# Segment sums of the state-space heads as two fp32r products: decay steps split into a high and a low part, spread over the triangle by VectorE and GpSimd

## The reference, cut to what matters

```python
cs = jnp.cumsum(dt * a.reshape(g, r), axis=2)
seg = cs[:, :, :, None] - cs[:, :, None, :]
decay_in = jnp.exp(jnp.where(lower, seg, -jnp.inf))
cb = jnp.einsum('bcqgn,bcsgn->bcqsg', cm, bm)
m = cb[..., None] * decay_in * dt[:, :, None]
y_diag = jnp.einsum('bcqsgr,bcsgrp->bcqgrp', m, x)
```

## Time and profile before

| what | value |
|---|---|
| median of 3 runs | 3071.8 us (3071.16 to 3074.44) |
| the profiled execution, its own time | 3071.51 us |
| its span | 3069.9 us |
| mean granted clock of PE | 0.964 of 2.4 GHz |

### The profile page before, as it was taken

The page is one execution under the profiler, slowest core; times in us unless marked ns, Lnnn a source line. Parts: engine busy times, 40 slices in busy tenths (PEclk is TensorE's granted clock), DMA queues, the critical chain, the costliest instruction groups (busy, mean ns, idle before and its releaser), DMA issues. The chain is left out here.

```text
span 3069.9 us, 50804 instructions
## 1 busy us (share of the span) xinstructions
PE 2810.0 (92%) x17878; PEld 2411.9 (79%) x17878; DVE 2146.2 (70%) x4117; ACT 1531.7 (50%) x2880; POOL 178.6 (6%) x180
## 2 busy tenths in 40 slices
PE   5999588899997993999999999999999999999993
PEld 4988355566665873999999999999999999999992
DVE  3565666666665447787787788788788778788773
ACT  3543344444444332555555555555555555555552
POOL 0000011001100000000000000000000000000001
PEclk8999799999999995999999999999999999999996
DMA  6121301121222433877777787777688678677754
GB/s 249 65 64 56 114 23 45 50 93 64 85 82 102 160 130 131 258 243 232 247 242 226 242 254 222 235 247 239 221 254 241 219 245 250 222 247 240 230 190 174
DMA packets 359719, 547.40 MB, mean 178 GB/s; under 512 B 14785, under 2 KB 287937, under 8 KB 359617
## 3 DMA queue, kind: packets, MB, share of 16 engines
q1 hardware_dynamic: 350720, 514.59, 50.6%
q0 software_dynamic: 8896, 31.46, 4.3%
HBM read 493.51 MB, written 52.49 MB: 178 GB/s over the span
## 5 line engine op out<-in xcount | busy, mean ns | idle before, releaser
L2531 PE MATMUL banks<-rowsT_parts,weights_high 128*128 128x384 f32 x4096 | 1184.0, 361 | 12.3 <-DVE hidden_parts L2462 7.3
L2532 PE MATMUL banks<-rowsT_parts,weights_low 128*128 128x192 f32 x4096 | 1026.3, 251 | 0.0
L2531 PEld LDWEIGHTS banks<-rowsT_parts,weights_high 128*128 128x128 f32 x4096 | 770.0, 188 | 21.5 <-DVE hidden_parts L2462 9.9
L2532 PEld LDWEIGHTS banks<-rowsT_parts,weights_low 128*128 128x128 f32 x4096 | 783.4, 191 | 1.4
L2542 PE MATMUL banks<-weights_high,hidden_parts 128*128 128x512 f32 x1536 | 435.5, 392 | 0.0
L2449 DVE TENSOR_TENSOR gate_up_sums<-banks,gate_up_sums 128x192 f32<-128x192 f32 x512 | 181.6, 355 | 327.7 <-ACT gate_up_sums L2367 327.7
L2367 ACT ACTIVATE gate_up_sums<-banks 128x192 f32<-128x192 f32 x512 | 165.0, 322 | 452.2 <-PE banks L2532 448.2
L2542 PEld LDWEIGHTS banks<-weights_high,hidden_parts 128*128 128x128 f32 x1536 | 283.4, 188 | 69.9
L2542 PE MATMUL banks<-weights_low,hidden_parts 128*128 128x512 f32 (+1 forms) x1024 | 319.6, 393 | 0.0
L2399 DVE TENSOR_TENSOR weights_low<-slab_up,weights_high 128x1024 fp32r<-128x1024 f32 x256 | 311.9, 1218 | 0.0
L2399 DVE TENSOR_TENSOR weights_low<-slab_down,weights_high 128x1024 fp32r<-128x1024 f32 x256 | 311.5, 1217 | 0.0
(11 more groups left out here) (288 smaller groups left out, 3754.1 us busy)
## 6 DMA issues: line engine op xcount, KB each, us to landing
slab_gate<-w_gate SPq DMA_DIRECT2D x128, 1024.0 KB, 5.4
slab_up<-w_up SPq DMA_DIRECT2D x128, 1024.0 KB, 7.3
slab_down<-w_down SPq DMA_DIRECT2D x128, 1024.0 KB, 4.9
arena_attend<-w_ada SPq DMA_DIRECT2D x8, 2048.0 KB, 7.9
arena_attend<-ssd_tiles SPq DMA_DIRECT2D x12, 992.0 KB, 9.5
arena_inputs<-w_ada SPq DMA_DIRECT2D x4, 2048.0 KB, 12.2
ssd_tiles<-arena_inputs SPq DMA_DIRECT2D x24, 256.0 KB, 2.0
mixed<-arena_attend SPq DMA_DIRECT2D x12, 512.0 KB, 2.6
```

The lines of the kernel that those rows point to most:

```text
L2531: nc.tensor.matmul(out[:, 0:2 * CT], w_hi[:, u, block], x[:, k, :], start=k == 0, stop=False)
L2532: mm = nc.tensor.matmul(out[:, 0:CT], w_lo[:, u, block], x[:, k, 0:CT], start=False, stop=k == KD - 1)
```

## The change

- The decay steps of the next tile are split by DVE in turn 4 (`steps`): `step_hi` is `dta` rounded to fp32r (128x16), `step_lo` is `dta` minus `step_hi`.
- `terms` spreads both parts over the triangle, so each engine makes two tensors of 128x1024 where it made one, with fp32r as their output type. DVE makes the one of the high part in turn 6, where its only one was, and the one of the low part at the end of turn 7. POOL makes both one after the other, and waits for `steps_done` of the next tile where it waited for the tile's transfer.
- Each of the four segment sums is two fp32r products that add up in PSUM, high and low, with a copy of the triangles in fp32r as the stationary operand. The copy is made once at the start.
- `r_sum`, the triangles and the steps have memory of their own, and the shared area is 2048 columns smaller.

```diff
-    r_sum = A.at(A_R, 2, NS, P)
+    r_sum = core.once("decay_steps", [P, 2, 2, NS, P], F32R)
+    turns_r = core.once("triangles", [P, 2, P], F32R)
+    step_hi = core.once("steps_high", [P, 2, 16], F32R)
+    step_lo = core.once("steps_low", [P, 2, 16])
...
         def _(pool):
             def terms(g, j):
 
-                wait_apart(pool, tile_in[j], turn_of(g, j) + 16, pool_turns)
+                wait_apart(pool, steps_done, g + 1, pool_turns)
                 wait_apart(pool, seg_mm, g * 4, pool_turns)
-                nc.gpsimd.tensor_tensor(r_sum[:, 1], core.masks[:, M_GE, :].unsqueeze(1).broadcast_to([P, NS, P]),
-                                        dta[j][:, 8:16].unsqueeze(2).broadcast_to([P, NS, P]),
-                                        ALU.mult).then_inc(terms_b, 1)
+                for part, steps in enumerate((step_hi[:].bitcast(F32), step_lo[:])):
+                    ins = nc.gpsimd.tensor_tensor(r_sum[:, part, 1], core.masks[:, M_GE, :].unsqueeze(1).broadcast_to([P, NS, P]),
+                                                  steps[:, j, 8:16].unsqueeze(2).broadcast_to([P, NS, P]), ALU.mult)
+                ins.then_inc(terms_b, 1)
...
-            def terms(g, j):
+            def steps(g, j):
 
                 dve.wait_ge(tile_in[j], turn_of(g, j) + 16)
+                if not early(g):
+                    dve.wait_ge(terms_b, g - 1)
+                nc.vector.tensor_copy(step_hi[:, j], dta[j]).then_inc(steps_high, 1)
+                dve.wait_ge(steps_high, g + 3)
+                nc.vector.tensor_tensor(step_lo[:, j], dta[j], step_hi[:, j].bitcast(F32), ALU.subtract).then_inc(steps_done, 1)
+
+            def terms(g, j, part):
+                dve.wait_ge(steps_done, g + 1)
                 dve.wait_ge(seg_mm, g * 4)
-                nc.vector.tensor_tensor(r_sum[:, 0], core.masks[:, M_LE, :].unsqueeze(1).broadcast_to([P, NS, P]),
-                                        dta[j][:, 0:8].unsqueeze(2).broadcast_to([P, NS, P]),
-                                        ALU.mult).then_inc(terms_f, 1)
+                nc.vector.tensor_tensor(r_sum[:, part, 0], core.masks[:, M_LE, :].unsqueeze(1).broadcast_to([P, NS, P]),
+                                        (step_hi[:].bitcast(F32), step_lo[:])[part][:, j, 0:8].unsqueeze(2)
+                                        .broadcast_to([P, NS, P]), ALU.mult).then_inc(terms_f, 1)
...
+                    for d in range(2):
+                        nc.vector.tensor_copy(turns_r[:, d], core.masks[:, (M_GT, M_LT)[d], :]).then_inc(steps_high, 1)
                     keys_dve(dve, lambda t: front(t + 3, lo, 0, 0))
-                    terms(lo, 0)
+                    steps(lo, 0)
+                    for part in range(2):
+                        terms(lo, 0, part)
                     front(Q_STATS, lo + 1, 1, 1)
...
                     if follows and h == 6:
-                        terms(g + 1, 1 - j)
+                        terms(g + 1, 1 - j, 0)
...
+                    if follows and h == 4:
+                        steps(g + 1, 1 - j)
+                    if follows and h == 7:
+                        terms(g + 1, 1 - j, 1)
                     if h == 4:
                         add_off(g)
...
                 d, grp = divmod(p, 2)
-                pe.wait_ge((terms_f, terms_b)[d], g + 1)
+                pe.wait_ge((terms_f, terms_b)[d], g + 1 if d else g * 2 + 2)
...
-                nc.tensor.matmul(b_y, core.masks[:, (M_GT, M_LT)[d], :],
-                                 r_sum[:, d, 4 * grp:4 * grp + 4, :].rearrange("p h q -> p (h q)"),
-                                 start=True, stop=True).then_inc(seg_mm, 1)
+                for part in range(2):
+                    mm = nc.tensor.matmul(b_y, turns_r[:, d, :],
+                                          r_sum[:, part, d, 4 * grp:4 * grp + 4, :].rearrange("p h q -> p (h q)"),
+                                          start=part == 0, stop=part == 1)
+                mm.then_inc(seg_mm, 1)
```

More of the change, by code:

```diff
@@ L181, in small, with once @@
         return self.stage.enter_context(self.nc.sbuf_tensor(name, shape, dtype))
-    def once(self, name, shape):
+    def once(self, name, shape, dtype=F32):
         if name not in self.kept:
-            self.kept[name] = self.small(name, shape)
+            self.kept[name] = self.small(name, shape, dtype)
         return self.kept[name]
@@ L228, in at @@
         return v.rearrange(f"p ({' '.join(names)}) -> p {' '.join(names)}", **dict(zip(names, dims)))
-ARENA = 48768
+ARENA = 46720
 A_NAT = 25984
@@ L1086 @@
 A_P, A_PT = 14848, 16896
-A_KN, A_QN = 18944, 47232
+A_KN, A_QN = 18944, 35072
 A_CN, A_CT2 = 20480, 21248
@@ L1091 @@
 A_QT, A_O = 30976, 33024
-A_R, A_E, A_XDT, A_Y, A_CBM = 35072, 37120, 39168, 40192, 42240
-A_REC, A_JUNKM = 42752, 46720
+A_E, A_XDT, A_Y, A_CBM = 37120, 39168, 40192, 42240
+A_REC, A_JUNKM = 42752, 36608
 A_KROT = A_NAT + NT * (NAT - QL)
@@ L1279, in mixers @@
         sem(n) for n in ("off_mm", "off_done", "diag_mm", "y_order", "y_gated", "y_sumsq", "y_rstd", "y_normed", "y_turned", "y_mixed"))
+    steps_high, steps_done = sem("triangles_and_steps_high"), sem("steps_split")
     pool_turns, dve_turns = sem("mix_pool_turns"), sem("mix_dve_turns")
@@ L1844, in first @@
                     pe.wait_ge(sem(name), hi)
+                if not r:
+                    pe.wait_ge(steps_high, 2)
                 scores(lo, 0, 0)
```

## The result

The changed kernel takes 3123.2 us in the median of 4 runs (3122.33 to 3127.86), against 3071.48 us before: a ratio of 1.0175 with a 95% interval of 1.0156 to 1.0193. The forecast was slower, 3089.5 us; the sign is right and the size is not. The loss is 51.7 us where 18 were forecast, and the time lies outside the range of 3066 to 3107 us. Two executions among all that were timed ran at a far lower granted clock from end to end (one of the kernel before, 9194.95 us, and one of experiment 4, 3539.09 us), and are left out of every comparison.

What follows compares the result with a forecast made beforehand. PE sets a tile's pace, except where DVE's chain before `values` does. 3071.5 - 17.2 (segment sums) + 29.7 (DVE held by POOL) + 0.5 (turn 6) + 5 (start) = 3089.5 us; 8-in-10 range 3066 to 3107.

Steps and rivals of the forecast that it cites:

- The bound and the place: In `attend`, PE sets a tile's pace, except before `values`, where DVE's gapless chain does; delays there are paid in full.
- POOL's terms at their new place: Beside `add_off` and `gate`, POOL's two terms hold DVE; about 2.7 us in 11 tiles, 29.7 us including the split.
- The segment sums on PE: An fp32r pair takes 0.46 us instead of 0.86 for fp32; gain 1.43 us per tile, 17.2 us for 12 tiles.
- The start: Split and extra terms before the first maximum make it 4.8 us late; +5 us taken, bounds 1.4 and 7.
- The maximum, the copy and PE's `values` follow by as much: After `gate` on DVE, its 2.73 us lateness passes on to PE's `values`; 11 x 2.7 = 29.7 us.
- The rivals: POOL's terms late (3072 us, 0.12), no hold (3059, 0.10), `gate`'s PSUM-reading instruction held too (3114, 0.06), no fp32r gain (3107, 0.06).
- POOL too late: In turns 4 and 5, POOL misses its first opening and holds only `gate`'s last instruction, 1.2 us; 3072 us, chance 0.12.
- a longer hold: In `gate`, the PSUM-reading instruction is held too, making the last one 5.0 us late; 3114 us, chance 0.06.
- a pair without gain: In the segment sums, the fp32r pair gains nothing between fp32 products; 3107 us, chance 0.06.

Runs made afterwards that it cites:

- experiment 4: The changed kernel with DVE's split moved from turn 4 to behind `gate` in turn 5: 3073.03 us, ratio 1.0004 to the kernel before.
- experiment 1: The changed kernel with DVE's split of the decay steps moved from turn 4 to the end of turn 3: 3067.31 us, ratio 0.9981.
- experiment 2: The changed kernel with PE repeating head 7's score product before `values`, twice more in request 1, five times more in request 0: 3092.49 us, ratio 1.0064.
- experiment 5: The kernel of experiment 1 with PE repeating head 7's score product twice before `values` in request 0: 3060.76 us, ratio 0.9956.
- experiment 6: The kernel of experiment 1 with each fp32r pair of the segment sums run twice: 3083.38 us, ratio 1.0033.
- experiment 3: The kernel before the change, single fp32 products kept, plus DVE's split in turn 4 and two fp32 POOL terms released by it: 3160.92 us.

## Why the prediction was right in its mechanism and wrong in its size

- **The bound and the place.** Right in the main. PE's added waits stand before `values`, behind DVE's chain of turns 4 and 5, and at the start (5.84 us ahead of the first turning, against 0.95); experiment 1 moves the loss away by moving two small instructions.
- **The term "POOL's terms at their new place".** Right in ten of the 11 tiles with a follower. 2.7 us per tile forecast; `values` waits 3.7 us where 0.98 stood (4.96 and 2.31 in request 0), and the step with the hold and no fall of the clock is 50.65 us (experiment 2) against 47.92 without the hold (experiment 1), 2.73 us. In tile 5 POOL came too late for L1617, and the wait grew by 1.1 us only.
- **The segment sums on PE.** Right, a little high: 1.43 us per tile forecast, 1.36 measured in experiment 1, with a pair of 0.55 us instead of 0.46.
- **The start.** About right in size, in part by luck: +5 forecast. The 5.0 us at the first `gate` are not the start alone, since they hold 1.9 us of tile 0's own split and hold. Ahead of the split of tile 0 the change is 3.1 us late, after tile 0's segment sums have given back some 1.4 us. That makes some 4.5 us. The first maximum is 2.9 us late (390.47 against 387.59) where 4.8 were forecast, because the first terms could start earlier than the forecast had them (384.58, not 386.20). The rest comes with a fall of the clock from about 390 to 397, which the forecast did not have.
- **The failed step** is what the forecast made of "The maximum, the copy and PE's `values` follow by as much": the delay holds, but the sum took it as the whole price, 11 x 2.7 = 29.7 us, and had no term for the granted clock. A wait of 3.7 us does not only cost what it lasts. PE's granted clock falls to 1.2 GHz behind it, for 10.2 us in each of tiles 6 to 10 and for 7 to 14 us in tiles 0 to 4, and in tiles 6 to 9 that is worth 3.9 us each (54.5 against 50.65). In all it is about 30.7 us, by experiment 2. The rows of the kernel before had shown the sign of it. The clock was at its lower level from 416 to 426, behind the wait before `values` of tile 0 of request 0, and the next step was 37.87 us against 34.28 of its neighbours:

```profile
416.00:420.00 4.00, 3.06 (x20) 2.36 (x21) 2.80 (x5) 2.97 (x11) 0.42 (x1) 0.52 0.74 254
```

  I read the clock from the page's slices of 77 us, in which it hardly shows; the 0.97 of request 0 in the earlier trace rows was the hint.
- **The rivals.** None of the four came true as a whole, and none of them was the clock. The first, POOL too late, came true in tile 5: POOL started 0.64 us after the split's end there, and 0.27 to 0.35 us in the other tiles, where it still had its turn before L1617.
- **The chances.** Slower had 0.71. The range took in the price of a longer hold and of a pair without gain, and no second consequence of the wait.

The Trainium skill, "TensorE: Matmul & The Clock Gate", Part 1, section HAM oscillation, describes a kernel that is slowed again and again since each wait lets the clock drop. By that rule the forecast would have carried such a term as soon as `values` was to wait 3.7 us per tile. The traces agree in kind (a fall of 10.2 us in each of tiles 6 to 10), and the clock also fell behind waits of 2.3 us (request 0 of experiment 1).

The 2.5 cycles per element that the prediction takes from the Trainium skill, "GPSIMD Engine Reference", stand in its section 2.1 Instruction dispatch, and section 3.1 has about 2.6. Both give more (an estimate of 2.13 and 2.22 us) than the 1.90 us that POOL's terms take when nothing holds them (experiment 1), so the row was the better price.

## What to carry to other kernels

Before an edit that makes TensorE stand for some microseconds in each turn of a loop, look at the granted clock in windows of a few microseconds around the longest waits that are there already, and give the fall of the clock a term of its own: here 2.7 us of delay became 6.6 in tiles 6 to 9. A GpSimd instruction and a VectorE instruction with two SBUF inputs take turns, so ask what a newly placed semaphore lets start beside the chain that the slowest engine waits for; moving the release by one turn was worth 56 us. And where a wait can't be removed, repeating a product that is there anyway kept the clock up at little cost in the chain, as long as the repeats were shorter than the wait (experiments 2 and 5).

## What the runs showed of the hardware that was not expected

- Less work on PE may make it slower: with the same 2.3 us wait, the clock fell behind each tile of request 0 when the segment sums took less time (experiment 1), behind tile 0 and not tiles 1 and 2 before, and behind fewer tiles when the pair was doubled (experiment 6). One profile of each kernel shows it; the cause is argued, not shown.
- Two kernels with the same code in the later stages differ there by 32.6 us (experiment 3): 100 instead of 40 packets in the instruction queue, some 1.8 us at one DVE line in 12 of 16 experts, and falls of PE's clock behind waits of at most 1.9 us in eight of them. That the packets are the cause was not tested.
- POOL's terms with fp32r output take the same 1.90 us as with fp32 output when nothing contends.
